# Up products with both parts of x as one operand of 512 columns, and two of four modulation pieces on GpSimd

## The reference

```python
mod = (silu_c @ w_mod[l] + b_mod[l]).reshape(B, 3 * N_SUB, 1, D)
x = macaron_half_ffn(x, norm_g[l, 0], *mod_terms(mod, 0), ffn_w_in[l, 0], ffn_w_out[l, 0])
# swiglu(h, w_in, w_out): a, b = split(h @ w_in); (silu(a) * b) @ w_out
```

## Time and profile before

| | |
|---|---|
| median of 3 runs | 3888.66 us |
| profiled execution | 3894.0 us |
| its span | 3892.3 us |
| mean granted TensorE clock | 0.987 |
| TensorE busy | 3789.0 us, 97% |
| VectorE busy | 2263.8 us, 58% |
| ScalarE busy | 1281.2 us, 33% |
| GpSimd busy | 253.0 us, 7% |
| HBM read | 656.94 MB, 169 GB/s over the span |

### The profile page before, as it was taken

One profiled execution on the slowest core, in us unless ns is written; L12 is line 12 of the kernel. 1 busy time (PEld: TensorE's weight loads), 2 busy tenths in 40 slices (PEclk: granted clock), 3 DMA queues, 4 the chain that ended last, 5 costly groups with the idle time before them and its releaser, 6 DMA issues.

```text
span 3892.3 us, 59720 instructions
## 1 busy us (share of the span) xinstructions
PE 3789.0 (97%) x24508; PEld 3400.3 (87%) x24508; DVE 2263.8 (58%) x3345; ACT 1281.2 (33%) x1758; POOL 253.0 (7%) x322
## 2 busy tenths in 40 slices
PE   7998999999999999999998999999999999999999
PEld 7987889998799985999987799999989599998698
DVE  5744568772477765786845578555534555551255
ACT  3322133331333334333322233434311333331133
POOL 0001300000000000000002200000000100000000
PEclk9998999999999999999998999999999999999999
DMA  8642067674376653766732177454621345463443
GB/s 278 235 146 84 11 220 240 212 239 142 134 243 217 232 183 116 249 229 216 238 95 81 44 243 239 164 202 147 202 79 49 114 162 195 163 200 120 162 162 108
DMA packets 453564, 661.06 MB, mean 170 GB/s; under 512 B 15288, under 2 KB 385299, under 8 KB 452904
## 3 DMA queue, kind: packets, MB, share of 16 engines
q1 hardware_dynamic: 432280, 579.48, 43.6%
q0 software_dynamic: 21072, 78.56, 6.2%
HBM read 656.94 MB, written 2.00 MB: 169 GB/s over the span
## 4 chain that ended last, share of the span: by engine, by line
PE 92%; DVE 4%; ACT 2%; issue 1%; SPq 0%; DMA 0%; POOL 0%; POOLq 0%; DVEq 0%; ACTq 0%
PE ps L678 14%; PE ps L680 14%; PE ps L679 14%; PE ps L701 6%; PE ps L702 6%; PE ps L703 6%; PE ps L1137 4%; PE ps L972 4%; PE ps L2789 3%; PE ps L1173 2%; PE ps L1328 1%; PE ps L1670 1%; PE ps L2509 1%; PE ps L2512 1%; PE ps L1250 1%; PE ps L1265 1%
## 5 line engine op out<-in xcount | busy, mean ns | idle before, releaser
L678 PE MATMUL ps<-parts 128*128 128x256 f32 x4576 | 1300.5, 284 | 4.2 <-DVE parts L869 4.2
L679 PE MATMUL ps<-parts 128*128 128x256 f32 x4576 | 1294.8, 283 | 0.0
L680 PE MATMUL ps<-parts 128*128 128x256 f32 x4576 | 1294.7, 283 | 0.0
L678 PEld LDWEIGHTS ps<-parts 128*128 128x128 f32 x4576 | 877.4, 192 | 13.2 <-issue 6.2
L679 PEld LDWEIGHTS ps<-parts 128*128 128x128 f32 x4576 | 877.5, 192 | 7.0
L680 PEld LDWEIGHTS ps<-parts 128*128 128x128 f32 x4576 | 877.4, 192 | 0.0
L624 DVE TENSOR_TENSOR parts<-ring,parts 128x2048 fp32r<-128x2048 f32 x286 | 654.9, 2292 | 209.1 <-ACT parts L613 207.6
L817 ACT ACTIVATE silu<-ps 128x256 f32<-128x256 f32 x286 | 110.0, 384 | 1478.5 <-PE ps L680 1478.5
L613 ACT ACTIVATE parts<-ring 128x2048 fp32r<-128x2048 f32 x286 | 545.7, 1910 | 38.2 <-DMA ring<-in_ffn_w_out 38.1
L881 DVE TENSOR_TENSOR silu<-silu,ps 128x256 f32<-128x256 f32 x286 | 119.7, 419 | 587.2 <-ACT silu L817 587.2
L701 PE MATMUL ps<-parts 128*128 128x512 f32 x1144 | 448.5, 392 | 0.0
(11 more groups left out here) (422 smaller groups left out, 3915.3 us busy)
## 6 DMA issues: line engine op xcount, KB each, us to landing
ring<-in_ffn_w_gu SPq DMA_DIRECT2D x176, 1024.0 KB
ring<-in_ffn_w_in SPq DMA_DIRECT2D x110, 1024.0 KB
ring<-in_ffn_w_down SPq DMA_DIRECT2D x88, 1024.0 KB
ring<-in_ffn_w_out SPq DMA_DIRECT2D x55, 1024.0 KB
ring<-in_gdn_w_in SPq DMA_DIRECT2D x32, 1024.0 KB
arena<-in_w_mod POOLq DMA_DIRECT2D x24, 1024.0 KB, 5.6
xn<-in_w_mod POOLq DMA_DIRECT2D x24, 1024.0 KB, 5.7
arena<-in_w_mod POOLq DMA_DIRECT2D x48, 512.0 KB, 8.8
```

The source lines that it names most:

```text
L678: nc.tensor.matmul(dst, w_u[:, m, :], h_hi[:, k, a:b], start=(k == 0), stop=False)
L679: nc.tensor.matmul(dst, w_u[:, m, :], h_lo[:, k, a:b], start=False, stop=False)
L680: ins = nc.tensor.matmul(dst, w_l[:, m, :], h_hi[:, k, a:b], start=False, stop=(k == KD - 1))
```

## The change

`up_products` takes `h_hi` and `h_lo` of a block as one moving operand: two runs of 256 columns in one of 512 (`h_pair`), so upper x upper lands in the bank's columns 0 to 255 and upper x lower in 256 to 511; the lower weights' product is added to the latter. Each side of a tile now fills a bank of its own, three banks in turn (`sum_bank`), and `up_done` counts sides. The halves are added after: ScalarE copies the second half to SBUF (`silu` for side 0, `up_low` for side 1), VectorE adds the first half from PSUM to it. ScalarE then takes the silu in place, and VectorE's product of silu and side 1 has both inputs in SBUF. TensorE waits at each side for the add that frees the bank.

Pieces 2 and 3 of each loop go to GpSimd (`mod_piece_pool`): one product of the whole 128 x 8 x 256 chunk with `m_s`, in place, then sums of halves with 4, 2 and 1 blocks of 256 columns. TensorE waits for them at the same places as before. In GpSimd's queue piece 2 stands behind the wait for piece 1 and the issue of `load_c`. Stages that use the buffers next wait for `m_pool`.

```diff
+    H_APART = pieces.at
...
         if f >= GU_SLOTS:
-            act.wait_ge(up_done, count(f - GU_SLOTS + 1, it, 2 * RING))
+            act.wait_ge(up_done, count(2 * (f - GU_SLOTS) + 2, it, 4 * RING))
...
-            if f >= UPB:
-                pe.wait_ge(act_done, count(f - UPB + 1, it, step))
...
+        def h_pair(k):
+            hi = h_hi[:, k, :]
+            return bass.AP(tensor=hi.tensor, offset=hi.offset, ap=[list(hi.ap[0]), [H_APART, 2], [1, T]])
...
             for side in range(2):
-                dst = ps[:, 4 + i % UPB, side * T + a:side * T + b]
+                if 2 * i + side >= 3:
+                    last = 4 * (f - 2) + 2 if side == 0 else 4 * (f - 1) + 1
+                    pe.wait_ge(a_parts, count(last, it, 4 * step))
+                both_parts, lower = ps[:, sum_bank(i, side), :], ps[:, sum_bank(i, side), T:2 * T]
...
-                    nc.tensor.matmul(dst, w_u[:, m, :], h_hi[:, k, a:b], start=(k == 0), stop=False)
-                    nc.tensor.matmul(dst, w_u[:, m, :], h_lo[:, k, a:b], start=False, stop=False)
-                    ins = nc.tensor.matmul(dst, w_l[:, m, :], h_hi[:, k, a:b], start=False, stop=(k == KD - 1))
+                    nc.tensor.matmul(both_parts, w_u[:, m, :], h_pair(k), start=(k == 0), stop=False,
+                                     skip_group_check=True)
+                    ins = nc.tensor.matmul(lower, w_l[:, m, :], h_hi[:, k, :], start=False, stop=(k == KD - 1),
+                                           skip_group_check=True)
+                ins.then_inc(up_done, 1)
...
-            nc.scalar.activation(silu[:, i % UPB, :], ps[:, 4 + i % UPB, 0:T], ACT.Silu).then_inc(silu_done, 1)
+            nc.scalar.activation(a, ps[:, sum_bank(i, 0), T:2 * T], ACT.Copy).then_inc(low_copied, 1)
+            act.wait_ge(a_parts, count(4 * f + 1, it, 4 * step))
+            nc.scalar.activation(a, a, ACT.Silu).then_inc(silu_done, 1)
+            act.wait_ge(up_done, count(2 * f + 2, it, 2 * step))
+            if f:
+                act.wait_ge(a_parts, count(4 * f - 1, it, 4 * step))
+            nc.scalar.activation(up_low[:, :], ps[:, sum_bank(i, 1), T:2 * T], ACT.Copy).then_inc(low_copied, 1)
...
+            dve.wait_ge(low_copied, count(2 * f + 1, it, 2 * step))
+            nc.vector.tensor_tensor(a, a, ps[:, sum_bank(i, 0), 0:T], ALU.add).then_inc(a_parts, 1)
+            dve.wait_ge(low_copied, count(2 * f + 2, it, 2 * step))
+            nc.vector.tensor_tensor(up_low, up_low, ps[:, sum_bank(i, 1), 0:T], ALU.add).then_inc(a_parts, 1)
             dve.wait_ge(silu_done, count(f + 1, it, step))
-            nc.vector.tensor_tensor(a, a, ps[:, 4 + i % UPB, T:2 * T], ALU.mult).then_inc(a_parts, 1)
+            dve.wait_ge(a_parts, count(4 * f + 2, it, 4 * step))
+            nc.vector.tensor_tensor(a, a, up_low, ALU.mult).then_inc(a_parts, 1)
...
+    def mod_piece_pool(pool, at, n, it):
+        done = KP * (M_HALF * at["ffn"] + n % 2)
+        w = m_w[M_PIECES[n][0] == "b"]
+        mod_loaded(pool, at, n, it)
+        nc.gpsimd.tensor_tensor(w, w, m_s[:, :, 0:1].to_broadcast([P, KD, MC]), ALU.mult).then_inc(m_pool, 1)
+        for i, half in enumerate((4, 2)):
+            pool.wait_ge(m_pool, done + i + 1 + it * (2 * KP))
+            nc.gpsimd.tensor_tensor(w[:, 0:half, :], w[:, 0:half, :], w[:, half:2 * half, :], ALU.add)\
+                .then_inc(m_pool, 1)
+        pool.wait_ge(m_pool, done + 3 + it * (2 * KP))
+        mod_acc_free(pool, at, n, it)
+        nc.gpsimd.tensor_tensor(m_acc[:, n, :], w[:, 0, :], w[:, 1, :], ALU.add).then_inc(m_pool, 1)
...
         with pool.Fori(0, ITERS - 1) as it:
-            free(it, 1)
+            pool.wait_ge(m_step, KD * (M_HALF * f + 2) + it * (KD * 2))
             load_c(it)
-            free(it, 2)
+            mod_piece_pool(pool, at, 2, it)
+            pool.wait_ge(m_pool, KP * (M_HALF * f + 1) + it * (KP * 2))
             load_b(1, it)
-            free(it, 3)
+            mod_piece_pool(pool, at, 3, it)
+            pool.wait_ge(m_pool, KP * (M_HALF * f + 2) + it * (KP * 2))
             load_a(1, it)
-        free(ITERS - 1, 1)
+        pool.wait_ge(m_step, KD * (M_HALF * f + 2 * ITERS))
         load_c(ITERS - 1)
+        mod_piece_pool(pool, at, 2, ITERS - 1)
+        mod_piece_pool(pool, at, 3, ITERS - 1)
...
-            pe.wait_ge(m_step, KD * (M_FFN * at["ffn"] + n + 1) + it * (KD * M_TURN))
+            step, each = (m_step, KD) if n < 2 else (m_pool, KP)
+            pe.wait_ge(step, each * (M_HALF * at["ffn"] + n % 2 + 1) + it * (each * 2))
```

More of the change, by code:

```diff
@@ L321, in square_act @@
             act.wait_ge(turned, NQ * n)
+        last = last_step(at) if at in STEPS else None
+        if q == 0 and is_ffn(last) and last["n"] < 8:
+            act.wait_ge(m_pool, KP * M_HALF * (last["ffn"] + 1))
         nc.scalar.activation(xn[:, t, cols], src[:, t, cols], ACT.Square, scale=float(D) ** -0.5,
@@ L656, in split_first_dve, with sum_bank @@
                 gu_lower_dve(dve, at, j)
+    up_low = arena[:, KD * CH:KD * CH + T]
+    def sum_bank(i, side):
+        return 4 + (2 * i + side) % 3
     def ffn_pe(pe, at):
@@ L664, in up_free, with up_products @@
             pe.wait_ge(gu_lower, count(f + 1, it, step))
[L665 to L668 removed]
+        def h_pair(k):
+            hi = h_hi[:, k, :]
+            return bass.AP(tensor=hi.tensor, offset=hi.offset, ap=[list(hi.ap[0]), [H_APART, 2], [1, T]])
+        def up_products(i, it=None, row=None):
             f = f0 + i
@@ L737, in ffn_pe @@
         up_free(0)
-        up_products(0, 0, T, row=1).then_inc(up_done, 1)
+        up_products(0, row=1)
         up(1)
@@ L813, in tile @@
         def tile(i, it):
-            act.wait_ge(up_done, count(f0 + i + 1, it, 2 * RING))
-            if f0 + i >= UPB:
-                act.wait_ge(act_done, count(f0 + i - UPB + 1, it, 2 * RING))
-            nc.scalar.activation(silu[:, i % UPB, :], ps[:, 4 + i % UPB, 0:T], ACT.Silu).then_inc(silu_done, 1)
+            f, step, a = f0 + i, 2 * RING, silu[:, i % UPB, :]
+            act.wait_ge(up_done, count(2 * f + 1, it, 2 * step))
+            if f >= UPB:
+                act.wait_ge(act_done, count(f - UPB + 1, it, step))
+            nc.scalar.activation(a, ps[:, sum_bank(i, 0), T:2 * T], ACT.Copy).then_inc(low_copied, 1)
[5 more added lines that the diff above has]
+            nc.scalar.activation(up_low[:, :], ps[:, sum_bank(i, 1), T:2 * T], ACT.Copy).then_inc(low_copied, 1)
             if i == 0 and it is None and at["n"] >= 8:
@@ L2255, in build @@
     M_FFN = M_TURN * ITERS
+    M_HALF = 2 * ITERS
+    KP = 4
     x_ctx = arena[:, 0:TT * D].rearrange("p (t d) -> p t d", t=TT)
@@ L2308, in gate_act, with mod_loaded, mod_acc_free @@
                              scale=GATES[at["kind"], at["n"]][3]).then_inc(gate_ready, 1)
+    def mod_loaded(eng, at, n, it):
+        f, chunk = at["ffn"], M_PIECES[n][0]
+        if chunk == "b":
+            eng.wait_ge(m_loaded[1], 16 * ITERS * f + 16 + it * 16)
+        else:
+            eng.wait_ge(m_loaded[0], 64 * ITERS * f + (32 if chunk == "a" else 64) + it * 64)
+    def mod_acc_free(eng, at, n, it):
+        before = M_FFN * at["ffn"] + n
+        if isinstance(it, int) and deferred(at):
+            eng.wait_ge(m_sum, 2 + before - 3 + it * M_TURN)
+        else:
+            eng.wait_ge(m_sum, 2 + before - 1 + it * M_TURN)
+    def mod_piece_pool(pool, at, n, it):
[10 more added lines that the diff above has]
+        nc.gpsimd.tensor_tensor(m_acc[:, n, :], w[:, 0, :], w[:, 1, :], ALU.add).then_inc(m_pool, 1)
     def mod_pool(pool, at):
@@ L2339, in mod_pool @@
         with pool.Fori(0, ITERS - 1) as it:
-            free(it, 1)
+            pool.wait_ge(m_step, KD * (M_HALF * f + 2) + it * (KD * 2))
             load_c(it)
-            free(it, 2)
+            mod_piece_pool(pool, at, 2, it)
+            pool.wait_ge(m_pool, KP * (M_HALF * f + 1) + it * (KP * 2))
             load_b(1, it)
-            free(it, 3)
+            mod_piece_pool(pool, at, 3, it)
+            pool.wait_ge(m_pool, KP * (M_HALF * f + 2) + it * (KP * 2))
             load_a(1, it)
-        free(ITERS - 1, 1)
+        pool.wait_ge(m_step, KD * (M_HALF * f + 2 * ITERS))
         load_c(ITERS - 1)
+        mod_piece_pool(pool, at, 2, ITERS - 1)
+        mod_piece_pool(pool, at, 3, ITERS - 1)
     def mod_tile_dve(dve, at, u, it):
-        f = at["ffn"]
-        for n, (chunk, cond, at_u) in enumerate(M_PIECES):
+        for n in range(2):
+            chunk, cond, at_u = M_PIECES[n]
             if at_u != u:
                 continue
-            before = M_FFN * f + n
-            if chunk == "b":
-                dve.wait_ge(m_loaded[1], 16 * ITERS * f + 16 + it * 16)
-            else:
-                dve.wait_ge(m_loaded[0], 64 * ITERS * f + (32 if chunk == "a" else 64) + it * 64)
-            if isinstance(it, int) and deferred(at):
-                dve.wait_ge(m_sum, 2 + before - 3 + it * M_TURN)
-            else:
```

(7 more changed lines are left out.)

16 lines of the change are left out of this document (7 added, 9 removed).

## The result

The changed kernel takes 4055.12 us (median of 4 runs, 4051.49 to 4057.88) against 3889.67 us (3886.79 to 3891.10) for the kernel before: ratio 1.042, 95% interval 1.041 to 1.044. It is slower by 4.2%, inside the range (3945 to 4115) and 34 us over the forecast of 4021. The profiled execution has a span of 4054.1 us for 3892.3, with a mean granted clock of 0.973 for 0.987.

A forecast was written before the change was run, and what follows sets the result against it. TensorE, busy for 97% of the span, was taken as the bound. Matmuls -53.5, waits +116, clock +42 and last loops +28 gave +132.5 us on 3894.0, so 4026.5; less 5.3 for the median, 4021 (range 3945 to 4115).

The forecast's parts named there:

- the walk: Timeline of one six-tile loop from up(0)'s end: TensorE waits 0.3 us for piece 1 and 6.5 for piece 2.
- 2 x 0.120 - 0.228: Up products: two 256-column matmuls less one of 512, 16 times a tile, saving 0.19 us a tile, 53.5 us in all.
- up tiles of 5.58 us: Expected sign in stages n >= 8, where no piece runs: shorter up tiles, making each stage 4 us shorter.
- rival (b): Up products: the pair operand gives no saving, the rest as forecast; 4075 us, chance 0.08.
- I cost all of it at nothing: Copies on ScalarE, adds on VectorE, three PSUM banks and the longer way to a_lo: hidden behind TensorE, 0 us.
- the price named for a lost cover: Longer way from up's end to a_lo: 0.45 us a tile at most if it were not hidden.
- The cover that I named: Way to a_lo: hidden by two tiles before down needs it, at the stage's end by 12 matmuls of 0.228 us.
- gu_lower, ready at 22.7: Walked loop: VectorE's gu_lower ready at +22.7 us, running from 27.1 to 29.4 between GpSimd's first two instructions.
- the signs of being right: Expected profile: 17 waits of 5 to 8 us at the product with ones, L624's maximum 4 to 7 us, clock 0.5 afterwards.
- rival (c): Loops: neither VectorE nor GpSimd waits for the other and the clock stays up; 3888 us, no change, chance 0.07.
- rows 10: Profile rows before the change: TensorE's clock at 0.50 after 4.12 and 5.23 us without work; 2.5 us added per wait.
- I take 4: Last loop of stages n = 0 to 6: TensorE's wait for gu_lower, between 0 and 13 us, taken as 4, seven times.

The follow-up runs named there:

- The up side alone: The kernel before with the 512-column operand, copies, adds and three banks; all four modulation pieces stay on VectorE: 3934.35 us, ratio 1.012.
- the run with the last sum first: The changed kernel with GpSimd's last sum of a piece made first and TensorE waiting for that alone; product and half sums follow: 4058.92 us.
- the pieces alone: The kernel before with pieces 2 and 3 moved to GpSimd; up products, silu and product as before: 3971.24 us.
- the run with half the product: The changed kernel with GpSimd's sums of 4 and 2 blocks left out and its product cut from 2048 to 1024 elements: 3880.46 us.

## Why the prediction was right, and where it was wrong

**The direction and its mechanism: right.** Two waits of TensorE a loop arise where the walk put them, and leaving out GpSimd's product and half sums takes the whole loss away. The walk up to GpSimd's product was exact: piece 1 ends at +19.78 (19.7 to 19.8), the product starts at +22.23 (22.2; the walk with turns starts it at 22.5). The 17 waits at the product with ones are there, and TensorE's next block waits for `gu_lower`.

**Saved matmul time: 53.5 us forecast, 32 measured.** The step that failed is 2 x 0.120 - 0.228. The 0.228 is the spacing among twelve 512-column products; beside a 256-column one it is 0.236, and the 256-column ones go at 0.117 each. A block's three took 0.360 and its two take 0.353: 0.113 us a tile, which the tiles of n >= 8 show (0.68 us less in six). The "up tiles of 5.58 us" that make a stage "4 us" shorter came out as 2.3 us a stage. The forecast missed this term by 21 us, rival (b), no saving, by 32.

**"I cost all of it at nothing" for the copies and adds: wrong.** The up side alone costs 37 us of span; with the 32 us that it saves, the adds and the longer way to `a_lo` cost some 69 us, 0.24 a tile (the price named for a lost cover was 0.45 at most). The cover that I named holds in a loop to within a microsecond but not at the stage's end, where the twelve matmuls ahead don't hide a VectorE that is behind.

**Waits of TensorE: 6.8 us a loop forecast, 4.4 measured.** That is the mean of the 17 loops; in most of them it is some 1.8 us for piece 2, 1.5 for `gu_lower` and 1.0 for the `gu_lower` behind piece 3, which the walk held to cost nothing. GpSimd's four instructions took 3.63, 3.82 (two) and 0.72 us, 8.2 with no turn given, where I had 8.9 and a turn of 2.3 for `gu_lower` between the first two. Piece 2 ends at +30.64 where the walk had 35.1 with turns and 31.4 alone. The failed step is "gu_lower, ready at 22.7": VectorE had not come that far. Its product L911, ready at +21.3 and so ahead of GpSimd's, was held to that one's end. The gaps between GpSimd's instructions then went to short instructions of VectorE, and `gu_lower` ran after the half sums, to +32.8. So its longest is 3.35 us, where the signs of being right asked for 4 to 7, and the longest wait at the product with ones is 3.8, where they asked for 5 to 8. That they take turns, as assumed, was right in kind: where a long one is queued (the run with the last sum first) it gets its turn.
**Clock: 2.5 us a loop forecast, 1.7 at most in the loop shown** (0.24, 0.50 and 0.11 of 2 us each, part of the first while TensorE is idle anyway), behind idle times of 1.74 and 1.52 us with four tiny matmuls between. Five of the 16 hardware loops lose twice that, so the mean is 2.2, near the forecast. Over the whole span the granted clock takes 58 us more than before (0.027 x 4054 for 0.013 x 3892, idle time included), some 22 of them in the last stretches. The rival (c) hoped that a wait shorter than those of rows 10 would keep the clock up; it did in no loop of the changed kernel (0.50 in 158 to 160), but it did in some of the pieces alone. There the one wait of 2.8 us in the first loop of n = 0 (to 97.8) and that in the second (to 155.1) have these rows:

```profile
98.00:100.00 2.00, 2.00 (x16) 2.00 (x16) 2.00 (x1) 0.00 (x0) 1.67 (x2) 0.82 0.03 4
100.00:102.00 2.00, 2.00 (x11) 2.00 (x11) 2.00 (x2) 0.00 (x0) 2.00 (x1) 0.50 0.94 311
...
154.00:156.00 2.00, 0.86 (x7) 0.86 (x8) 1.97 (x3) 0.00 (x0) 1.18 (x3) 1.00 0.00 0
156.00:158.00 2.00, 2.00 (x19) 2.00 (x18) 2.00 (x2) 0.00 (x0) 1.98 (x2) 1.00 0.32 45
```

**Last stretch: 7 x 4 us forecast, about 70 measured** (65.8 for the stages n = 0 to 6, and 4 for the saving inside). Of the 0 to 13 us that the walk left open, "I take 4" was too low: TensorE waits 4.6 us for `gu_lower(5)`, until 216.38, with the clock at 0.50 behind it, and `a_lo` is late for the down products, by 2.8 us in n = 1, 3 and 5 and 0.5 in the even ones, which the walk did not have.

**The sum.** For + 132.5 us: - 32 (for - 53.5), + 128 for 17 loops (for 158), + 70 for the last stretches (for 28), - 4 between stages: + 162. Three terms missed by 20 to 40 us each with changing signs, so the nearness of the total is partly luck. Of the 7.5 us that a loop costs (128 / 17), waits and clock make 6.6; the rest was not traced. The 5.3 us taken off for the median were not there either: the changed kernel's profiled run and its median agree.

**What the parts' sum hid.** Why do 37 and 77 make 162? On VectorE's account, relative to before: the pieces alone add 323 us of holding and take off 190 of steps, + 133; the up side alone adds 240 of adds; both 370. The losses before the saved matmul time are 77, 69 and 194. One slack of VectorE that both parts share would explain that together they cost more than apart, but not that 133 us cost more than 240: in the pieces alone TensorE also waits for the late piece itself (44.9 us). Among the runs with the up side and some of GpSimd's work the account fits: 81, 170, 218, 223 and 370 us more on VectorE cost -1, 19, 42, 49 and 194. So the shared slack is argued and not shown, and the run with half the product shows that it differs by stretch.

## What to carry to other kernels

Before moving work from VectorE to GpSimd, count what VectorE loses: each of its instructions with two inputs in SBUF, and its casts, may stand still for a whole GpSimd instruction. Here 190 us of steps were taken off it and 320 us of standing still put on. An addition on an engine that is busy for 60% is only free where that engine has slack at that point of the schedule, so price it at the end of the stage and in the fullest tile; and price a longer matmul from its spacing in the sequence where it will stand.
